# Block inverses of a recurrent scan: one product with a masked sum, ScalarE copies in place of VectorE adds, and two directions interleaved on the array

## The chip, the cores and the metric

The kernel runs on one core of a Trainium2 chip. The metric is the device time of one execution in microseconds (us). Three runs of the kernel before gave 3592.19, 3597.78 and 3598.36 us; their median, 3597.78 us, is the time before.

## The reference, cut to what matters

The program computes three transformer blocks on a sequence of 512 tokens of width 1024. The third has a recurrent mixer with 8 heads of width 64 in two directions over 528 positions (16 leading ones and 512 tokens). In each direction and head a 64x64 state S obeys, from one position to the next,

```python
def rwkv7_step(S, inp):
    r, w, k, v, kk, kka = inp
    sa = jnp.einsum('dbhij,dbhj->dbhi', S, -kk)
    S = S * w[..., None, :] + sa[..., :, None] * kka[..., None, :] + v[..., :, None] * k[..., None, :]
    y = jnp.einsum('dbhij,dbhj->dbhi', S, r)
    return S, y
```

The kernel takes 64 positions at once (a chunk). Within a chunk the values `sa` solve a triangular 64x64 system, whose matrix is I minus the strictly triangular matrix N of products of `kk` and `kka`. So each chunk needs, for 8 heads and 2 directions, the inverse P of such a matrix. It is the same for any state, and is worked out one chunk ahead of its use.

## The kernel before, in words

The program is one hand-ordered stream of instructions for each engine, tied by semaphores. Matrix products of the large projections take most of it; the change is in one stage, `RwkvScan` (lines 2345 to 2654), whose instructions lie between 2780.74 us and 3017 us of the profiled span.

The stage has one step for the 16 leading positions (called chunk -1, one direction only) and eight for the chunks 0 to 7. `steps()` gives pairs (c, n): in one step the state is carried over chunk c, while the matrices and the inverse of chunk n = c + 1 are made. The pairs are (none, -1), (-1, 0), (0, 1), ... (6, 7), (7, none).

A head is a 64x64 matrix, so a product of heads uses a quarter of the 128x128 array: which one is fixed by the half of the partitions (0 to 63 or 64 to 127) that the operands lie in and by the half that the result goes to. The trace writes such an operation as 64*64. Each float32 product shows as two matmul rows, so the 16 products of a group for both directions (4 columns of heads, 2 halves, 2 directions) are "x32", and those of one direction "x16". `quads` (line 2366) lists, for each direction and half, where the channels lie (F) and where the positions lie (t): in direction 0 both are in the same half, in direction 1 in opposite ones. A product from F to t thus uses all four quarters over the two directions, while one from t to t uses two, the two on the diagonal.

The order of TensorE in a step (line 2527 on), with the lines of the products: `grams` makes N and its transpose (2448, 2459); `right_side` (2468, 2474, 2478) and `early_sums` (2486, 2488) serve chunk c; `below` (2513) and `doubled` (2520, 2523) are a level of the inverse of chunk n, and there are five levels (block sizes 2, 4, 8, 16, 32); between the first ones stand `solution` (2493) and `late_sums` (2500, 2502) of chunk c, `pairs` with k (2459) and `fill`, which transposes three operands by products with the identity (2440).

A level before the change, per direction: `below` makes N P; VectorE multiplies it by the level's mask into `c_y` (line 2588); `doubled` makes P y (2520) and the same for the transposed inverse (2523); VectorE adds both products to `c_p` (lines 2595 and 2597). The last level makes only the first and adds it into `c_pf`. All products are from t to t.

VectorE also masks the grams (2568), adds the identity to the inverse of block size 2 and its transpose, four additions (2581), updates the state (2605, 2609), and from chunk 4 on adds the outputs (2618). ScalarE copies the right side, the solution and the transposed operands out of the accumulators (2384), the outputs of chunks 0 to 3 (2410), and after chunk -1 does two sigmoids.

Of the kernel before, what the change touches and what calls it, by code (L numbers as in the profile page):

```python
# [1305 lines left out]
class LowerBounds(Stage):  # L1306


    def dve(self, K, P):
# [4 lines left out]
        P.e.tensor_tensor(t[:, 16:24], b, m, ALU.subtract).then_inc(P.sem("lb_shifted"), P.adds("lb_shifted"))  # L1314
        P.e.wait_ge(P.sem("lb_exp"), P.due("lb_exp"))
# [7 lines left out]
    def act(self, K, P):  # L1323
        P.e.wait_ge(P.sem("lb_shifted"), P.due("lb_shifted"))
        P.e.activation(K.lbt[:, 8:24], K.lbt[:, 8:24], ACT.Exp).then_inc(P.sem("lb_exp"), P.adds("lb_exp"))
# [216 lines left out]
class BiasTable(Stage):  # L1542
# [4 lines left out]
    def dve(self, K, P):  # L1547
# [8 lines left out]
        P.e.reduce_sum(K.lamt[:, 0:2], K.lam_prod[:, :].rearrange("p (a c) -> p a c", a=2), AX.X).then_inc(P.sem("lambda_dots"), P.adds("lambda_dots"))  # L1556
        P.e.wait_ge(P.sem("lambda_exps"), P.due("lambda_exps"))
# [4 lines left out]
    def act(self, K, P):  # L1562
        P.e.wait_ge(P.sem("lambda_dots"), P.due("lambda_dots"))
        P.e.activation(K.lamt[:, 2:4], K.lamt[:, 0:2], ACT.Exp).then_inc(P.sem("lambda_exps"), P.adds("lambda_exps"))
# [780 lines left out]
class RwkvScan(Stage):  # L2345
# [35 lines left out]

    def act(self, K, P):
        def take(dst, bank, half, n):
            return P.e.activation(dst[:, 0:n, :, :], self.two(K, bank, half, n), ACT.Copy)

# [6 lines left out]
        for c, n in self.steps():  # L2392
            if c is not None:
# [6 lines left out]
                if c < 0:  # L2400
                    finish_loads(K, P, K.loads3d)
                    P.e.activation(K.z_gate[:, 0, :], K.z_gate[:, 0, :], ACT.Sigmoid)
                    P.e.activation(K.z_gate[0:32, 1, :], K.z_gate[0:32, 1, :], ACT.Sigmoid)
                    P.e.preload_act_table_set("natural_log_exp_and_others")
                if c == 7:
                    start_loads(K, P, K.loads3e)
                if 0 <= c < 4:
                    P.e.wait_ge(P.sem("state_ready"), P.due("state_ready", 0))
                    for d in range(2):
                        last = P.e.activation(K.ys[:, :, self.tokens(c, d)], self.two(K, 4, 1, 2)[:, d], ACT.Copy)  # L2410
                    last.then_inc(P.sem("y_taken"), P.adds("y_taken"))
            if n is not None:
                m = self.dirs(n)
# [6 lines left out]
    def pe(self, K, P):  # L2420
# [84 lines left out]
        def one_way(n, d):  # L2505
            return [(F, t, q, 64 * q) for q in range(4) for e, F, t in self.quads(n) if e == d]
# [1123 lines left out]
```

## Time and profile before

| | |
|---|---|
| median of three runs | 3597.78 us |
| lowest, highest run | 3592.19, 3598.36 us |
| span of the profiled execution | 3592.5 us |
| own time of the profiled execution | not recorded apart from its span |
| TensorE busy | 3438.7 us, 96% |
| VectorE busy | 1946.5 us, 54% |
| ScalarE busy | 1275.7 us, 36% |
| mean granted TensorE clock | 0.988 of full speed |

The rows of the trace have the start in us, the duration in us, the engine (PE is TensorE's matmuls, PEld its weight loads, DVE is VectorE, ACT is ScalarE), the line, the operation, what it writes and reads, the shape and the count. In brackets stands how long the engine was idle before it, and what released it.

### The profile page before, as it was taken

The page shows a single profiled execution, that of the slowest core. Times are in us where ns is not written, and L with a number is a line of the kernel's source. Part 1 is how long each engine was busy: PE and PEld are TensorE (multiplying, and loading weights), DVE is VectorE, ACT ScalarE, POOL GpSimd, SP SyncE. Part 2 cuts the span into 40 slices and gives each one's busy share as a digit, 9 for nine tenths or more (in the row PEclk, how much of TensorE's full clock was granted, in tenths as well). Part 3 has the DMA queues.
Part 4 walks back from the last instruction along what each step waited for, and adds up shares of the span by engine and source line. Part 5 has one row for each costly group of instructions (what it writes and reads, how often), then busy time and mean ns, then how long its engine had stood idle before and what let it go on. Part 6 is the DMA issues. An engine that isn't in the chain of part 4 may idle for free.

```text
span 3592.5 us, 54754 instructions
## 1 busy us (share of the span) xinstructions
PE 3438.7 (96%) x22789; PEld 2842.5 (79%) x22789; DVE 1946.5 (54%) x2646; ACT 1275.7 (36%) x1637; POOL 0.2 (0%) x4
## 2 busy tenths in 40 slices
PE   9999999999999999999999989999899888999998
PEld 7788888887788877778887768888787886888887
DVE  4566736436574654575344455344667666755434
ACT  3474424334442332453223343222532113643223
POOL 0000000000000000000000000000000000000000
PEclk9999999999999999999999999999999999999999
DMA  4102222221123222113222212222224001122221
GB/s 157 59 1 94 94 99 100 94 94 47 59 94 105 94 86 94 58 59 99 100 94 94 93 48 93 101 99 94 92 98 148 18 4 32 66 82 98 98 97 70
DMA packets 50429, 297.06 MB, mean 83 GB/s; under 512 B 6847, under 2 KB 7871, under 8 KB 17348
## 3 DMA queue, kind: packets, MB, share of 16 engines
q1 hardware_dynamic: 39376, 269.92, 22.1%
q10 hardware_dynamic: 10868, 24.41, 1.9%
q8 instruction: 148, 2.42, 0.3%
q14 instruction: 37, 0.30, 0.0%
HBM read 283.99 MB, written 10.33 MB: 82 GB/s over the span
## 4 chain that ended last, share of the span: by engine, by line
PE 87%; DVE 8%; ACT 3%; issue 1%; DMA 0%; ACTq 0%; DVEq 0%
PE PS L353 14%; PE PS L354 14%; PE PS L355 14%; PE PS L478 7%; PE PS L479 7%; PE PS L480 7%; PE PS L1995 2%; PE PS L1996 2%; PE PS L1997 2%; PE PS L2520 1%; PE PS L1300 1%; PE PS L1280 1%; PE PS L2523 1%; PE PS L2513 1%; PE PS L3012 1%
## 5 line engine op out<-in xcount | busy, mean ns | idle before, releaser
L172 DVE TENSOR_TENSOR WL<-W,WH 128x2048 fp32r<-128x2048 f32 x249 | 570.7, 2292 | 685.8 <-ACT WH L162 680.1
L162 ACT ACTIVATE WH<-W 128x2048 fp32r<-128x2048 f32 x249 | 476.3, 1913 | 1059.5 <-PE PS L480 553.3
L353 PE MATMUL PS<-XH,WH 128*128 128x512 f32 x2144 | 838.1, 391 | 4.3 <-issue 4.3
L355 PE MATMUL PS<-XH,WL 128*128 128x512 f32 x2144 | 835.2, 390 | 0.0
L354 PE MATMUL PS<-XL,WH 128*128 128x512 f32 x2144 | 835.1, 390 | 0.0
L353 PEld LDWEIGHTS PS<-XH,WH 128*128 128x128 f32 x2144 | 403.1, 188 | 94.0 <-issue 10.6
L354 PEld LDWEIGHTS PS<-XL,WH 128*128 128x128 f32 x2144 | 403.2, 188 | 84.2 <-issue 1.0
L355 PEld LDWEIGHTS PS<-XH,WL 128*128 128x128 f32 x2144 | 403.0, 188 | 84.1
L752 DVE TENSOR_TENSOR PS<-PS,R 128x512 f32<-128x512 f32 x248 | 171.0, 696 | 445.1 <-PE PS L355 440.8
L478 PE MATMUL PS<-HH,WH 128*128 128x512 f32 (+1 forms) x960 | 374.6, 390 | 1.2
L479 PE MATMUL PS<-HL,WH 128*128 128x512 f32 (+1 forms) x960 | 373.6, 389 | 0.0
L480 PE MATMUL PS<-HH,WL 128*128 128x512 f32 (+1 forms) x960 | 373.5, 389 | 0.0
L478 PEld LDWEIGHTS PS<-HH,WH 128*128 128x128 f32 x960 | 180.2, 188 | 43.0 <-issue 5.8
L480 PEld LDWEIGHTS PS<-HH,WL 128*128 128x128 f32 x960 | 180.2, 188 | 37.4
L479 PEld LDWEIGHTS PS<-HL,WH 128*128 128x128 f32 x960 | 180.2, 188 | 37.0
L1028 ACT ACTIVATE CV<-PS,params 128x512 f32<-128x512 f32 x88 | 68.0, 780 | 228.4 <-DVE PS L752 228.4
L1995 PE MATMUL PS<-XHM,WH 128*128 128x264 f32 (+1 forms) x416 | 138.4, 333 | 7.7 <-DVE slots L2199 7.7
L1996 PE MATMUL PS<-XLM,WH 128*128 128x264 f32 (+1 forms) x416 | 136.8, 329 | 0.0
L1997 PE MATMUL PS<-XHM,WL 128*128 128x264 f32 (+1 forms) x416 | 136.5, 328 | 0.0
L478 PE MATMUL PS<-XH,WH 128*128 128x512 f32 x256 | 100.2, 392 | 1.0 <-issue 1.0
L479 PE MATMUL PS<-XL,WH 128*128 128x512 f32 x256 | 99.9, 390 | 0.0
L480 PE MATMUL PS<-XH,WL 128*128 128x512 f32 x256 | 99.8, 390 | 0.0
(490 smaller groups left out, 4577.9 us busy)
## 6 DMA issues: line engine op xcount, KB each, us to landing
W<-in_weights SPq DMA_DIRECT2D x254, 1024.0 KB, 4.9
gate_spill<-slots ACTq DMA_DIRECT2D x16, 256.0 KB, 2.0
gates<-gate_spill ACTq DMA_DIRECT2D x2, 2048.0 KB
x_spill<-X ACTq DMA_DIRECT2D x1, 2048.0 KB, 8.8
X<-x_spill ACTq DMA_DIRECT2D x1, 2048.0 KB
out<-X ACTq DMA_DIRECT2D x8, 256.0 KB, 2.1
W<-in_weights SPq DMA_DIRECT2D x2, 512.0 KB, 5.2
X<-in_x ACTq DMA_DIRECT2D x4, 256.0 KB, 7.5
```

What stands on the lines that cost most here:

```text
L162: P.e.activation(K.WH[:, s, :], K.W[:, s, :], ACT.Copy).then_inc(P.sem("hi_ready"), P.adds("hi_ready"))
L172: P.e.tensor_tensor(K.WL[:, s, :], K.W[:, s, :], K.WH[:, s, :].bitcast(F32), ALU.subtract).then_inc(P.sem("weights_split"), P.adds("weight ...
L353: P.e.matmul(out, wh[:, k, c], xh[:, k, r], start=(k == 0), stop=False)
L354: P.e.matmul(out, wh[:, k, c], xl[:, k, r], start=False, stop=False)
L355: last = P.e.matmul(out, wl[:, k, c], xh[:, k, r], start=False, stop=(k == KT - 1))
L478: P.e.matmul(out, K.WH[:, s, c], h, start=(first and kk == 0), stop=False)
L479: P.e.matmul(out, K.WH[:, s, c], l, start=False, stop=False)
L480: last = P.e.matmul(out, K.WL[:, s, c], h, start=False, stop=(last_panel and kk == 1))
L752: P.e.tensor_tensor(ps, ps, K.RB[:, :], ALU.mult).then_inc(P.sem("tile_scaled"), P.adds("tile_scaled"))
L1995: P.e.matmul(out, wh[:, k, c], K.XHM[:, k, r], start=(k == 0), stop=False)
L1996: P.e.matmul(out, wh[:, k, c], K.XLM[:, k, r], start=False, stop=False)
L1997: last = P.e.matmul(out, wl[:, k, c], K.XHM[:, k, r], start=False, stop=(k == KT - 1))
```

## The change

What it does:

- `below`, `doubled` and their order: the mask of a level now includes the diagonal, and `c_n` is N + I, so that the masked product y is I plus the block, and P y is the new inverse itself. Nothing has to be added: ScalarE copies the new inverse (`grown`) and its transpose (`turned`) out of the accumulators.
- In direction 1 the intermediate product and the transposed inverse lie in the other half of the partitions (`seat`), so `below` and `grown` of direction 1 use the two quarters off the diagonal. `grown_beside_below` alternates the products of `grown` of one direction with those of `below` of the other.
- `turned` writes to the banks 2 and 3, and `grams` makes 8 further products (16 rows) that put the first transposed matrix of direction 1 into that other half.
- VectorE's order: `begin` masks `c_n` first, and adds the identity in three wide additions (in both directions at once) in place of four; the mask of the first level stands before that of `c_rb`; all additions to `c_p` and `c_pf` are gone.
- ScalarE's order: the copies of the inverse stand between those it had; the sigmoids of the step c = -1 stand at the end of the step.
- Four semaphores of short exponentials elsewhere become two by shared names. This alters no order.

The core of the diff (as it was, with parts left out):

```diff
@@ act
+        def grown(d, final=False):
+            dst = K.c_pf if final else K.c_p[:, 0]
+            P.e.wait_ge(P.sem("inverse_done"), P.due("inverse_done"))
+            P.e.activation(dst[:, d, :, :], self.two(K, 0, 0, 2)[:, d], ACT.Copy).then_inc(P.sem("inverse_ready"), P.adds("inverse_ready"))
+
+        def turned(d):
+            P.e.wait_ge(P.sem("turned_done"), P.due("turned_done"))
+            P.e.activation(K.c_p[:, 1, d, :, :], self.two(K, 2, 1, 2)[:, d], ACT.Copy).then_inc(P.sem("turned_ready"), P.adds("turned_ready"))
+
+        def level(n):
+            for d in range(n):
+                grown(d)
+                turned(d)
...
+            if n is not None:
+                level(self.dirs(n))
...
             if n is not None:
                 m = self.dirs(n)
+                level(m)
                 P.e.wait_ge(P.sem("rows_done"), P.due("rows_done"))
                 take(K.c_bT, 6, 0, m)
+                if full:
+                    level(m)
+                else:
+                    grown(0, True)
                 take(K.c_kT, 6, 1, m).then_inc(P.sem("rows_ready"), P.adds("rows_ready"))
+                if full:
+                    level(m)
+                    grown(0, True)
+                    grown(1, True)
                 P.e.wait_ge(P.sem("rows_done"), P.due("rows_done"))
                 take(K.c_v, 6, 0, m).then_inc(P.sem("rows_ready"), P.adds("rows_ready"))
@@ pe
             for d, F, t, q, cols in each(c):
                 mm(K.PS[t, d, cols], src(c, d, "a", F, q), src(c, d, "b", F, q), start=True, stop=True)
+                if d:
+                    mm(K.PS[F, 0, 256 + 64 * q:320 + 64 * q], src(c, d, "a", F, q), src(c, d, "b", F, q), start=True, stop=True)
             pairs(c, "b", "a")
...
+        def grown_beside_below(n, d, first=False):
+
+            P.e.wait_ge(P.sem("below_ready"), P.due("below_ready"))
+            if not first:
+                P.e.wait_ge(P.sem("turned_ready"), P.due("turned_ready"))
+            P.e.wait_ge(P.sem("inverse_ready"), P.due("inverse_ready"))
+            for (t, h, q, at), (t2, h2, q2, at2) in zip(heads(n, d), heads(n, 1 - d)):
+                out = mm(K.PS[t, d, at:at + 64], K.c_p[h, 1, d, q, :], K.c_y[h, d, q, :], start=True, stop=True)
+                new = mm(K.PS[h2, 1 - d, at2:at2 + 64], K.c_n[t2, 1 - d, q2, :], K.c_p[t2, 0, 1 - d, q2, :], start=True, stop=True)
+            out.then_inc(P.sem("inverse_done"), P.adds("inverse_done"))
+            new.then_inc(P.sem("below_done"), P.adds("below_done"))
+
+        def turned(n, d):
+            for t, h, q, at in heads(n, d):
+                last = mm(K.PS[h, 2 + d, 256 + at:320 + at], K.c_y[h, d, q, :], K.c_p[h, 1, d, q, :], start=True, stop=True)
+            last.then_inc(P.sem("turned_done"), P.adds("turned_done"))
...
+            right_side(c)
+            early_sums(c)
+            below(n, 0)
+            solution(c)
+            grown_beside_below(n, 0, first=True)
+            late_sums(c)
+            turned(n, 0)
+            for level in range(4):
+                grown_beside_below(n, 1, first=(level == 0))
+                if level == 0:
+                    P.e.wait_ge(P.sem("grams_masked"), P.due("grams_masked", 2))
+                    pairs(n, "k", "a")
+                turned(n, 1)
+                grown_beside_below(n, 0)
+                if level == 3:
+                    break
+                turned(n, 0)
+                if level == 0:
+                    fill(("b_rows", "k_rows"), n, ("grams_masked",))
+                elif level == 2:
+                    fill(("v_rows",), n, ("rows_ready",))
+            grown(n, 1)
+            P.e.wait_ge(P.sem("inverse_ready"), P.due("inverse_ready", 2))
@@ dve
+            masked(K.c_n, self.two(K, 0, 0, n), K.c_strict[:, 0:n, :], n)
+            masked(K.c_p[:, 0], self.two(K, 6, 0, n), K.c_first[:, 1:1 + n, :], n).then_inc(P.sem("grams_masked"), P.adds("grams_masked"))
+            masked(K.c_p[:, 1], self.one(K, 0, n), K.c_first[:, 0:n, :], n).then_inc(P.sem("dve_order"), P.adds("dve_order"))
+            eye = K.c_eye[:, :].rearrange("p (a n) -> p a n", a=1).broadcast_to([128, 4 * n, 64])
+            wide = lambda x: x[:, 0:n].rearrange("p d q n -> p (d q) n")
+            P.e.wait_ge(P.sem("dve_order"), P.due("dve_order", 0))
+            e.tensor_tensor(wide(K.c_n), wide(K.c_n), eye, ALU.add)
+            e.tensor_tensor(wide(K.c_p[:, 0]), wide(K.c_p[:, 0]), eye, ALU.add).then_inc(P.sem("inverse_ready"), P.adds("inverse_ready", n))
+            e.tensor_tensor(wide(K.c_p[:, 1]), wide(K.c_p[:, 1]), eye, ALU.add)
...
             begin(m)
+            below(m, 0)
             if full:
                 masked(K.c_rb[n % 2], self.two(K, 6, 1, m), K.c_incl[:, 0:m, :], m).then_inc(P.sem("grams_masked"), P.adds("grams_masked"))
-            below(m, 0)
-            doubled(m)
...
             below(m, 1)
             if full:
                 masked(K.c_rk, self.two(K, 6, 1, m), K.c_incl[:, 0:m, :], m).then_inc(P.sem("grams_masked"), P.adds("grams_masked"))
-            doubled(m)
             below(m, 2)
-            doubled(m, not full)
             if full:
                 below(m, 3)
-                doubled(m)
                 below(m, 4)
-                doubled(m, True)
```

## Rows read from the trace of the kernel before

**Rows 1.** The page: its head.

```profile
span 3592.5 us, 54754 instructions
```

**Rows 2.** The page: chain of work that ended last, by engine.

```profile
PE 87%; DVE 8%; ACT 3%; issue 1%; DMA 0%; ACTq 0%; DVEq 0%
```

**Rows 3.** Timeline: first product of steps n = -1, 0, 1, and of the last.

```profile
2780.74 0.54 PEld L2448 LDWEIGHTS PS<-c_meta 64*64 64x64 f32 x16 [1.77 <-ACTq L101]
...
2797.92 0.69 PE L2448 MATMUL PS<-ar 64*64 64x64 f32 x32 [0.58 <-ACT c_v L2384]
...
2821.84 0.69 PE L2448 MATMUL PS<-ar 64*64 64x64 f32 x32 [0.52 <-DVE c_pf L2597]
...
3010.76 1.15 PE L2468 MATMUL PS<-c_v,c_ak 64*64 64x64 f32 x32 [0.52 <-DVE c_pf L2597]
```

**Rows 4.** Timeline of one step (c = 2, n = 3) from its start, products and masks.

```profile
2876.05 0.56 PEld L2448 LDWEIGHTS PS<-ar 64*64 64x64 f32 x32 [0.66 <-DVE c_pf L2597]
...
2876.51 0.87 PEld L2459 LDWEIGHTS PS<-ar 64*64 64x64 f32 x32
...
2877.34 1.06 PEld L2468 LDWEIGHTS PS<-c_v,c_ak 64*64 64x64 f32 x32
...
2877.69 1.29 DVE L2568 TENSOR_TENSOR c_p<-PS,masks 128x512 f32<-128x512 f32 x2 [1.69 <-PE PS L2459]
...
2879.20 0.60 PEld L2478 LDWEIGHTS PS<-c_s,ar 64*64 64x64 f32 x32
...
2879.61 1.43 DVE L2581 TENSOR_TENSOR c_p<-c_p,wide_consts 128x256 f32<-128x256 f32 x4
...
2880.65 1.02 PEld L2513 LDWEIGHTS PS<-c_p,c_n 64*64 64x64 f32 x32
```

**Rows 5.** The same step: the state's update and the wait behind it.

```profile
2886.71 0.69 DVE L2605 TENSOR_TENSOR c_s<-c_s,PS 128x512 f32<-128x512 f32 x1 [0.75 <-PE PS L2502]
...
2889.30 0.55 PEld L2520 LDWEIGHTS PS<-c_y,c_p 64*64 64x64 f32 x16 [1.06 <-DVE c_y L2588]
```

**Rows 6.** The same step: the operands' transposes and one level.

```profile
2891.11 1.07 PEld L2440 LDWEIGHTS PS<-square_consts,ar 64*64 64x64 f32 x64
...
2892.09 1.02 PEld L2513 LDWEIGHTS PS<-c_p,c_n 64*64 64x64 f32 x32
...
2893.38 0.54 PEld L2520 LDWEIGHTS PS<-c_y,c_p 64*64 64x64 f32 x16 [0.27 <-DVE c_y L2588]
...
2895.71 1.16 PEld L2513 LDWEIGHTS PS<-c_p,c_n 64*64 64x64 f32 x32
```

**Rows 7.** Timeline: from a product through VectorE's mask to the next product.

```profile
2873.64 0.54 PEld L2513 LDWEIGHTS PS<-c_p,c_n 64*64 64x64 f32 x16 [0.40 <-DVE c_p L2597]
...
2874.37 0.42 DVE L2588 TENSOR_TENSOR c_y<-PS,masks 128x256 f32<-128x256 f32 x1 [0.45 <-PE PS L2513]
...
2874.84 0.55 PEld L2520 LDWEIGHTS PS<-c_y,c_p 64*64 64x64 f32 x16 [0.20 <-DVE c_y L2588]
```

**Rows 8.** ScalarE's copies: the 128x256 one by groups, a wide one and its reader.

```profile
L2410 ACT ACTIVATE ys<-PS 128x256 f32<-128x256 f32 x8 | 2.6, 381 | 16.7 <-DVE c_s L2609 16.7
...
3015.54 0.60 ACT L2384 ACTIVATE c_u<-PS 128x512 f32<-128x512 f32 x1 [1.55 <-PE PS L2493]
...
3016.19 0.56 PEld L2500 LDWEIGHTS PS<-c_rb,c_u 64*64 64x64 f32 x32 [0.84 <-ACT c_u L2384]
```

**Rows 9.** Waits of TensorE from 2780 to 3020 us: one cause.

```profile
PE PS L2493 <- issue: 2.4, 4, 0.8
```

**Rows 10.** Step n = -1: the product behind VectorE's longest queue.

```profile
2791.50 0.67 PEld L2520 LDWEIGHTS PS<-c_y,c_p 64*64 64x64 f32 x16 [2.79 <-DVE c_y L2588]
```

**Rows 11.** Stretches: from:to, length, PE, PEld, DVE, ACT, POOL busy, clock, DMA.

```profile
2790.00:2792.00 2.00, 0.49 (x14) 0.50 (x16) 1.45 (x3) 0.00 (x0) 0.00 (x0) 0.97 0.13 16
2792.00:2794.00 2.00, 2.00 (x44) 2.00 (x42) 0.75 (x2) 0.00 (x0) 0.00 (x0) 0.50 0.86 287
...
2877.00:2904.00 27.00, 24.55 (x930) 23.44 (x924) 17.29 (x42) 3.54 (x7) 0.00 (x0) 1.00 0.02 4
```

More of the change, by code:

```diff
@@ L2392, in act @@
         for c, n in self.steps():
+            full = n is not None and n >= 0
             if c is not None:
@@ L2503, in late_sums @@
             last.then_inc(P.sem("state_done"), P.adds("state_done"))
-        def one_way(n, d):
-            return [(F, t, q, 64 * q) for q in range(4) for e, F, t in self.quads(n) if e == d]
-        def below(n):
-            for d in range(self.dirs(n)):
-                P.e.wait_ge(P.sem("inverse_ready"), P.due("inverse_ready"))
-                for F, t, q, at in one_way(n, d):
-                    last = mm(K.PS[t, d, at:at + 64], K.c_n[t, d, q, :], K.c_p[t, 0, d, q, :], start=True, stop=True)
-                last.then_inc(P.sem("below_done"), P.adds("below_done"))
@@ new lines, in below, with grown @@
+        def below(n, d):
+            P.e.wait_ge(P.sem("inverse_ready"), P.due("inverse_ready"))
+            for t, h, q, at in heads(n, d):
+                last = mm(K.PS[h, d, at:at + 64], K.c_n[t, d, q, :], K.c_p[t, 0, d, q, :], start=True, stop=True)
+            last.then_inc(P.sem("below_done"), P.adds("below_done"))
+        def grown(n, d, first=False):
+            P.e.wait_ge(P.sem("below_ready"), P.due("below_ready"))
+            if not first:
+                P.e.wait_ge(P.sem("turned_ready"), P.due("turned_ready"))
+            for t, h, q, at in heads(n, d):
+                last = mm(K.PS[t, d, at:at + 64], K.c_p[h, 1, d, q, :], K.c_y[h, d, q, :], start=True, stop=True)
+            last.then_inc(P.sem("inverse_done"), P.adds("inverse_done"))
@@ L2539, in pe @@
                 continue
-            below(n)
-            if c is not None:
-                solution(c)
-            doubled(n)
-            if c is not None:
-                late_sums(c)
-            P.e.wait_ge(P.sem("grams_masked"), P.due("grams_masked", 2 if full else 1))
-            pairs(n, "k", "a")
-            below(n)
-            doubled(n)
-            fill(("b_rows", "k_rows"), n, ("grams_masked",))
-            below(n)
-            doubled(n, not full)
-            fill(("v_rows",), n, ("rows_ready",))
@@ L3160, in level @@
         return (row // (2 * b) == col // (2 * b)) & (lo // b % 2 == 0) & (hi // b % 2 == 1)
-    masks = [strict[d] for d in (1, 0, 1)] + [level(d, 1) for d in (1, 0, 1)] + [level(d, b) for b in (2, 4, 8, 16, 32) for d in range(2)]
+    masks = [strict[d] for d in (1, 0, 1)] + [level(d, 1) for d in (1, 0, 1)] + [level(d, b) | (row == col) for b in (2, 4, 8, 16, 32) for d in range(2)]
     more = [strict[d] | (row == col) for d in range(2)] + [row == col]
```

102 lines of the change are left out of this document (43 added, 59 removed).

## The prediction

> **What bounds the kernel now.** The head of the page gives the span, 3592.5 us [rows 1]. It is 0.15% below the median of the runs, 3597.78 us, so a difference worked out in the profile is subtracted from the median as it stands. The chain of work that ended last is 87% TensorE, 8% VectorE, 3% ScalarE [rows 2]; nearly all of TensorE's part lies in projections that the change doesn't touch. The timeline then finds the stage: its first product starts at 2780.74, the first of step n = 0 at 2797.92, of n = 1 at 2821.84, of the last step at 3010.76 [rows 3]. So step n = -1 takes 17.18 us, n = 0 23.92, and the seven steps n = 1 to 7 188.92, 26.99 each. The last step has no inverse and is unchanged.
>
> Inside a step TensorE is the bound by instructions rather than by waits: 24.55 us busy of 27, at the full clock (1.00, the 2.4 GHz level) [rows 11]. What a group costs depends on its quarters. Between 2879.20 and 2880.65 stand three groups of 32 rows between channels and positions (four quarters): 0.48 us each, and `grams` takes 0.46 for 32. Two groups of 32 from t to t (two quarters) take 1.86 us from 2877.34 to 2879.20, 0.93 each [rows 4]; 16 such rows hence take 0.46. The inverse is of that kind: a level in steady state lasts 2895.71 - 2892.09 = 3.62 us [rows 6] with 96 such rows, 2.8 us, besides 0.47 of a transposing group and waits. VectorE sets the end only in the opening (masks, additions) and behind the state's update, where TensorE waits 1.06 us [rows 5].
>
> **The change, walked through one step** (c = 2, n = 3; times from its start).
>
> *Opening.* `grams` gets 16 more rows, on the diagonal, which direction 0 uses too: 32 rows for two quarters, 0.93 instead of 0.46. With the 0.83 of line 2459 [rows 4] it ends at 1.76. VectorE started 1.64 after the step's start [rows 4], now 2.1. Three masks take 2877.69 to 2879.61, 1.92 us [rows 4], as before: 4.0. Then the wide additions replace four of 128x256, which took 1.43. No row has a 128x512 addition out of SBUF; it lies between one narrow one, 0.42, and two, 0.84 [rows 7], and I take the 0.69 of line 2605, same size [rows 5]. The first two are needed: 1.3, inverse ready at 5.35 (4.9 to 5.7). TensorE arrives at 1.76 + 3.31 = 5.07, so it waits 0.3.
> `below` for one direction 0.46, `solution` 0.93: 6.75. The alternating group has 32 rows on all four quarters, the pattern and banks of the `grams` group: 0.46, 7.2. `late_sums` needs ScalarE's copy of the solution. Before, 64 rows of `doubled` (1.86 us) covered it. A product group's start to the reader's start is about 0.73 for 16 rows in two quarters [rows 7], ScalarE's wide copy 0.60 and 0.05 to the reader [rows 8]: 7.6, so 0.4 of wait is uncovered. Late sums 0.95, `turned` 0.46: 9.0. Alternating group 0.46, `pairs` 0.83: 10.3.
>
> *Middle.* Before, VectorE's update of the state began at 2886.71, 10.66 after the start. Now it can begin at 8.8. From there to the product that it held up were 2.59 us [rows 5], of which a wide mask takes 0.64, a level's mask and its reader 0.47 [rows 7], leaving 1.5: ready at 10.3. So the wide mask of the second grams waits for `pairs` (10.3 + 0.35 = 10.65), and the next alternating group starts at 10.65 + 0.64 + 0.47, about 11.7. TensorE idles 1.0 there. VectorE then has this direction's mask, the other's at 11.7 + 0.73 (to 12.9) and the mask of `c_rk` (to 13.5), which frees the bank for `fill`: a new wait of 0.9, since `turned` ended at 12.65. Fill takes 0.98 [rows 6]: 14.5.
>
> *Levels.* From here each half level is latency: group start to mask 0.73, mask and reader 0.47, together 1.20 (2873.64 to 2874.84) [rows 7]. ScalarE's copy beside it is no later: 0.73 + 0.38 [rows 8] + 0.05 to 0.12. `turned` (0.46) and its copy fit in the next half. Three halves: 18.15; then `turned`, fill of v and start of the next, 1.45; two more halves: 22.0 for the last `grown`. It ends the step with 0.73, then ScalarE: the last inverse and behind it the copy of v, which `grams` waits for, 0.3 + 0.60 + 0.05. Step: 23.7. To this come pauses without a releaser ("issue"), 2.4 us over the stage at `solution` alone [rows 9], 0.3 a step; both ends for a step are 0 and 0.8, I take 0.6: 24.3. From c = 4, VectorE adds outputs before the wide mask, two of 128x256 at 0.34 and 0.42 by the four of 1.43 [rows 4]: 0.76, of which 0.35 is slack in the wait for `pairs`: 0.4 for three steps.
>
> *Sum.* Seven steps: 188.9 - 7 x 24.3 - 1.2 = -17.6 us. Step n = 0 has a shorter opening (one direction of c): by the same walk 23.0, -0.9. Its two sigmoids move behind its copies, under the next opening, where ScalarE has nothing to do until the right side is ready at 4.4: they cost nothing, and about 1 us once if that cover fails. Step n = -1: VectorE's long split of a weight panel stood behind `doubled` and held TensorE 2.79 us [rows 10]; now it runs beside `doubled`. -2.4, bounds 0 and -4. The added ScalarE work, 18 copies of 0.38 in a step, is on an engine that was busy 3.54 of 27 us [rows 11]. The two renamed semaphores cost nothing: same order. Total -20.9 us: 3577 us.
>
> **One rule against it.** In the `grams` group, two quarters of different row halves write the same bank, and four run together at 0.46 us for 32 rows [rows 4]. The Trainium skill ("TensorEngine Tiling (Array Packing)", section "Gotcha 1: PSUM Pressure") says that different row tiles cannot access the same bank at once. By that rule the alternating group, which has both halves in each of two banks, would gain nothing over two quarters; the trace disagrees, and so it is a rival with a small chance.
>
> **Rivals.**
> *The alternating groups don't overlap (slower).* Place: nine groups a step. Price: 0.93 in place of 0.46; eight are on the path, 3.7 us a step, 30 us: 3607 us. From 5.6 slow groups of the nine no gain is left, and from 7.5 it is slower by over 0.2%. For it: the mixed order (two products of different kinds) is in no row. Against it: the `grams` rows. Chance 0.04.
> *The clock falls in the new gaps.* The longest wait of the steady steps in the rows is 1.06 us [rows 5]. Now it works 0.9 us in the last 2.9 of a step, and idles twice in the middle. In step n = -1 the clock was 0.97 while TensorE was busy 0.49 of 2 us, and then 0.50 (the 1.2 GHz level) over the next 2 us, in which it was busy throughout [rows 11]. The row bounds the length of such a fall by 2 us from below; taken as 3, an estimate, half is lost, 1.5. At the end of seven steps that is 10.5: 3588 us, still faster. Chance 0.20. In two places of each step it would be 21, no change, 3598: 0.05.
> *ScalarE becomes the releaser.* If its copy comes 0.2 late in each half level, 9 x 0.2 x 8 = 14: 3591, within the bound of no change by a hair. Chance 0.05.
> *More comes.* If pauses vanish in the new waits and fill isn't held: 0.6 + 0.9 in seven steps, 10 more: 3566. Chance 0.10.
> That the change doesn't do what it says: the counts in the diff match (10 groups of `below`, 10 of `grown`, 8 of `turned` in a step, as before), so no chance of its own.
>
> **Numbers.** Forecast 0.56, the rivals 0.44. About 0.2% (7.2 us) is what a measurement of this kernel can tell from no change. Faster: 0.56 + 0.20 + 0.10, 0.86; same 0.09; slower 0.05. The range reaches from 3566 to the clock's case, 3589.
>
> **What would show it.** Steps of about 24.3 us instead of 27.0; the alternating lines 0.46 us from group to group's end; half levels 1.2 us apart, released by `c_y` of VectorE; a wait of `late_sums` for ScalarE near 0.4; one of `fill` near 0.9; the first `below` waiting 0.3 for the addition; TensorE's busy time in a step near 19 us. A clock under 1.00 in stretches at the start of steps would show the clock's case; alternating groups of 0.93 the rule; a longest wait on a copy, ScalarE's. Anything outside the stage that moved would make the prediction wrong in kind.

## The result, and the profile after

Nine executions of each kernel, alternating on one chip: 3606.17 us median after the change (3599.68 to 3614.0), 3595.45 before (3591.19 to 3598.36). The ratio is 1.0033 [1.0024, 1.0042]: the change makes the kernel slower by 10.7 us. 3577 us were forecast.

The page of the kernel after: its head, busy time by engine, and the chain by engine.

```profile
span 3604.0 us, 55035 instructions
...
PE 3425.8 (95%) x22917; PEld 2825.3 (78%) x22917; DVE 1897.2 (53%) x2490; ACT 1329.1 (37%) x1786; POOL 0.2 (0%) x4
...
PE 87%; DVE 8%; ACT 3%; issue 1%; DMA 0%; ACTq 0%; DVEq 0%
```

TensorE is busy 13 us less than before, although it has 128 product rows more, and the span is 11.5 us longer: what was saved in busy time came back as idle time, and more. The timeline of the kernel after says where. These rows correspond to [rows 3]: the first product of step n = -1, of n = 0, of n = 1, and of the last step.

```profile
2782.23 0.56 PE L2478 MATMUL PS<-c_meta 64*64 64x64 f32 x12 [1.34 <-ACTq L101]
...
2796.51 0.35 PE L2478 MATMUL PS<-ar 64*64 64x64 f32 x8 [0.57 <-ACT c_v L2388]
...
2824.29 0.50 PE L2478 MATMUL PS<-ar 64*64 64x64 f32 x8 [1.06 <-ACT c_v L2388]
...
3023.40 1.15 PE L2500 MATMUL PS<-c_v,c_ak 64*64 64x64 f32 x32 [1.02 <-ACT c_pf L2393]
```

Step n = -1 takes 14.3 us (17.18 before), n = 0 27.8 (23.92), the seven steps n = 1 to 7 199.1 (188.92). That is -2.9, +3.9 and +10.2, together +11.2 of the 11.5 us between the two spans: the difference lies in the stage, and nearly all of it in the steady steps.

For these I compare stretches of six steps in the view by stretches. Each runs from ScalarE's copy of `c_v` in step n = 0 to the same copy six steps later; that copy lies some 6 us ahead of a step's end before the change and at its end after it, which leaves the mean step as it is. The columns are those of [rows 11]. First the kernel before, then the one after.

```profile
2815.50:2977.55 162.05, 143.71 (x5384) 136.25 (x5382) 105.15 (x251) 19.90 (x39) 0.00 (x0) 1.00 0.02 4
```

```profile
2823.56:2993.86 170.30, 131.82 (x5472) 121.20 (x5472) 68.88 (x136) 61.81 (x151) 0.00 (x0) 0.97 0.02 4
```

The mean step is 27.0 us before and 28.4 after. TensorE's busy time fell by 2.0 us a step and VectorE's from 17.5 to 11.5, much as the change means it to. A step has 897 product rows before and 912 after (5384 and 5472 by six). Now the waits in these two stretches, first before, then after (us in total, times, longest).

```profile
PE PS L2520 <- DVE c_y L2588: 7.4, 7, 1.6
PE PS L2448 <- DVE c_pf L2597: 3.1, 6, 0.5
PE PS L2493 <- issue: 2.4, 4, 0.8
...
PE PS L2513 <- issue: 1.1, 2, 0.7
```

```profile
PE PS L2478 <- ACT c_v L2388: 6.6, 6, 1.3
PE PS L2562 <- issue: 4.5, 7, 1.0
PE PS L2470 <- DVE c_rk L2626: 4.2, 6, 0.7
PE PS L2561 <- issue: 4.2, 5, 1.4
PE PS L2561 <- DVE c_y L2645: 4.0, 5, 1.1
PE PS L2551 <- DVE c_y L2645: 3.4, 6, 0.6
PE PS L2568 <- issue: 2.9, 4, 1.1
PE PS L2470 <- issue: 1.7, 2, 0.9
...
```

Waits for an engine grew from 12.1 us to 19.4 over six steps, foreseen in kind. The rows "issue", in which TensorE waits for nothing that the profile shows, grew from 5.1 to 16.6 (all rows summed), which wasn't foreseen. I call these rows pauses. One step of the kernel after (c = 1, n = 2, from 2852.63 to 2879.83) shows where they stand.

```profile
2852.63 0.35 PE L2478 MATMUL PS<-ar 64*64 64x64 f32 x8 [1.06 <-ACT c_v L2388]
...
2860.31 0.57 PE L2532 MATMUL PS<-c_rb,c_u 64*64 64x64 f32 x23 [0.24 <-ACT c_u L2388]
...
2861.32 0.38 PE L2532 MATMUL PS<-c_rb,c_u 64*64 64x64 f32 x9 [0.44 <-issue]
...
2865.23 0.39 PE L2568 MATMUL PS<-c_p,c_y 64*64 64x64 f32 x7 [1.08 <-issue]
...
2867.36 1.16 PE L2470 MATMUL PS<-square_consts,ar 64*64 64x64 f32 x64 [0.69 <-DVE c_rk L2626]
...
2868.96 0.21 PE L2561 MATMUL PS<-c_y,c_p 64*64 64x64 f32 x1 [0.33 <-issue]
```

Two more, of 0.42 and 1.01 us, follow at 2872.67 and 2876.47. The five pauses make 3.3 us of this step of 27.20 us. They come every 3.8 us, in the middle of groups (after 23 of the 32 rows of line 2532), whatever the line. That spacing has one counterpart in the profile: the queue of instruction packets. Its row for the stretch 2823.56 to 2993.86 of the kernel after (packets, MB, share):

```profile
q8 instruction: 43, 0.70, 1.7%
```

43 packets of 16 KB in 170.3 us: one per 3.96 us. 5472 product rows and 5472 weight loads in 43 packets are 254.5 instructions in each, so I take 256 to a packet, 64 bytes each: 128 product rows with their weight loads. The kernel before has 42 in 162.05 us, one per 3.86 us:

```profile
q8 instruction: 42, 0.69, 1.8%
```

Hence the theory that I put to the test, called FEED in the expectations: TensorE's instructions arrive at a rate of about one packet per 3.4 to 4 us, 27 to 31 ns a product row. In two quarters a row takes 29 ns [rows 4], so by this theory the kernel before ran at the rate of arrival and showed hardly a pause; in four quarters it takes 14.4 ns, and then TensorE outruns its instructions. Its rivals: WAITS, the longer chain of copies and masks sets the step and the pauses are incidental; and the clock, which was at its lower level at some step starts (below).

### The profile page after: what moved, and what is told of

Read it like the earlier page. It is cut to its first block, busy times and chain, and to the rows that moved or that the text cites. A ratio compares the mean times of both kernels' runs of the same rounds, so it can differ in the third digit from the quotient of the medians.

```text
span 3604.0 us, 55035 instructions
## 1 busy us (share of the span) xinstructions
PE 3425.8 (95%) x22917; PEld 2825.3 (78%) x22917; DVE 1897.2 (53%) x2490; ACT 1329.1 (37%) x1786; POOL 0.2 (0%) x4
## 4 chain that ended last, share of the span: by engine, by line
PE 87%; DVE 8%; ACT 3%; issue 1%; DMA 0%; ACTq 0%; DVEq 0%
PE PS L353 14%; PE PS L355 14%; PE PS L354 14%; PE PS L478 7%; PE PS L480 7%; PE PS L479 7%; PE PS L1995 2%; PE PS L1996 2%; PE PS L1997 2%; PE PS L1300 1%; PE PS L1280 1%; PE PS L2561 1%; PE PS L3053 1%; PE PS L3055 1%; PE PS L3054 1%
```

## The experiments

Each difference is to the kernel before on the same chip; the kernel after stands at +10.7 us. The last five columns are of a six-step stretch, cut in the same way; pauses, waits and the time at half clock are us over the six steps. The stretch is of one execution, which for `in_turn` lay 4.2 us and for `tuned` 4.5 us below the median of its kernel, so their mean steps may be on the low side. The run `feed` has no row: it was executed once, at 3695.74 us, and only its trace is read.

| kernel | median us | ratio to before | difference | mean step | product rows a step | pauses | other waits | time at half clock |
|---|---|---|---|---|---|---|---|---|
| before | 3595.45 | | | 27.0 | 897 | 5.1 | 12.1 | 0 |
| after | 3606.17 | 1.0033 [1.0024, 1.0042] | +10.7 | 28.4 | 912 | 16.6 | 19.4 | 10.2 |
| wide_turned | 3596.14 | 0.9999 [0.9990, 1.0008] | +0.5 | 27.1 | 816 | 9.4 | 21.7 | 13.7 |
| in_turn | 3604.96 | 1.0025 [1.0016, 1.0035] | +9.4 | 28.3 | 912 | 8.2 | 19.7 | 10.2 |
| warm_ends | 3605.63 | 1.0027 [1.0018, 1.0036] | +10.0 | 28.1 | 918 | 18.7 | 10.0 | 0 |
| before_more | 3621.16 | 1.0074 [1.0058, 1.0089] | +26.2 | 29.8 | 1025 | 17.2 | 12.6 | 0 |
| wide_before | 3587.58 | 0.9977 [0.9967, 0.9986] | -7.4 | 25.7 | 801 | 2.0 | 10.3 | 0 |
| wide_all | 3578.55 | 0.9946 [0.9930, 0.9961] | -16.4 | 24.7 | 600 | 2.6 | 22.3 | 3.4 |
| tuned | 3596.14 | 0.9999 [0.9990, 1.0008] | +1.2 | 27.1 | 914 | 24.5 | 8.4 | 3.4 |
| in_place | 3589.70 | 0.9992 [0.9983, 1.0001] | -2.3 | 26.2 | 897 | 4.2 | 8.3 | 0 |
| before_tuned | 3584.60 | 0.9981 [0.9972, 0.9990] | -7.4 | 26.0 | 897 | 1.9 | 8.2 | 0 |
| wide_in_turn | 3577.13 | 0.9957 [0.9942, 0.9973] | -14.8 | 24.2 | 600 | 0.8 | 23.2 | 0 |

### feed: the rate by itself

Four blocks of 384 products each, with nothing to wait for, stand ahead of the stage's first step; their results are not used.

```diff
         P.e.wait_ge(P.sem("meta_staged"), P.due("meta_staged"))
+        H = self.HALVES
+        for i in range(384):
+            mm(K.PS[H[(i // 2) % 2], 6 + (i % 2 != (i // 2) % 2), 0:64], K.c_meta[H[i % 2], 0, 0, :], K.c_meta[H[i % 2], 1, 0, :], start=True, stop=True)
+        for i in range(384):
+            mm(K.PS[H[i % 2], 6, 0:64], K.c_meta[H[i % 2], 0, 0, :], K.c_meta[H[i % 2], 1, 0, :], start=True, stop=True)
...
```

The third block has 8 columns on four quarters, the fourth 128.

> The kernel after with four blocks of 384 extra 64x64 products ahead of the scan (1536 TensorE rows each, a weight load and a matmul counted as one row each; results unused): (1) four quarters, 64 columns; (2) two quarters, 64 columns; (3) four quarters, 8 columns; (4) four quarters, 128 columns. Theory FEED (TensorE's instructions arrive at no more than 256 rows, one 16 KB instruction packet, in about 3.4 us, 13.3 ns a row): block 1 about 20 us, block 2 about 22 us, block 3 about 20 us, block 4 about 20 us, and packets 3.4 us apart in all four. Theory ARRAY (the rate of short bursts, 0.46 us for 32 matmul rows in four quarters, holds): block 1 about 11 us, block 2 about 22 us, block 3 below 11 us, block 4 about 20 us; packets 1.9 us apart in block 1.

The timeline of the first block (four quarters, 64 columns, 768 product rows):

```profile
2781.70 2.66 PE L2574 MATMUL PS<-c_meta 64*64 64x64 f32 x164 [1.34 <-ACTq L101]
2785.73 2.09 PE L2574 MATMUL PS<-c_meta 64*64 64x64 f32 x128 [1.36 <-issue]
2789.20 2.09 PE L2574 MATMUL PS<-c_meta 64*64 64x64 f32 x128 [1.38 <-issue]
2793.22 2.09 PE L2574 MATMUL PS<-c_meta 64*64 64x64 f32 x128 [1.93 <-issue]
2796.96 2.09 PE L2574 MATMUL PS<-c_meta 64*64 64x64 f32 x128 [1.65 <-issue]
2800.98 1.56 PE L2574 MATMUL PS<-c_meta 64*64 64x64 f32 x91 [1.93 <-issue]
```

The four blocks by stretches (the clock is the third column from the end):

```profile
2781.70:2802.30 20.60, 12.36 (x765) 11.66 (x768) 0.00 (x0) 1.91 (x1) 0.00 (x0) 1.00 0.18 56
2802.30:2826.90 24.60, 23.31 (x788) 22.74 (x780) 0.00 (x0) 0.00 (x0) 0.00 (x0) 1.00 0.02 5
2826.90:2848.10 21.20, 19.34 (x778) 18.95 (x778) 0.00 (x0) 0.00 (x0) 0.00 (x0) 0.58 0.02 5
2848.10:2870.60 22.50, 22.50 (x772) 22.27 (x771) 0.00 (x0) 0.00 (x0) 0.00 (x0) 0.94 0.02 4
```

This shows what FEED says, if not at the 3.4 us that it named: bursts of exactly 128 rows, 2.09 us each, then a pause, 3.81 us from burst to burst on average ((2800.98 - 2785.73) / 4), with no semaphore in sight. The block takes 20.6 us, 27 ns a row, where 768 rows at 14.4 ns would be 11. The second block (two quarters) took 24.6 us, the third, of 8 columns and at a mean clock of 0.58, 21.2, the fourth, of 128, 22.5. The second and the fourth had been expected at 22 and 20 by both theories and don't tell them apart; the first and the third do. An eighth of the columns isn't done sooner, and a clock near the lower level doesn't make it later: it is the number of instructions that counts. Two quarters lose only 4 us to four.

The trace also holds the start and the end of each packet's transfer, and they tie the pauses to the packets. In the first block the transfers end at 2784.17, 2787.86, 2791.81, 2795.64 and 2799.62, and the five bursts start 1.56, 1.34, 1.41, 1.32 and 1.36 us later. In the stretch of the kernel after, each of the 24 pauses ends 1.27 to 1.59 us after the end of a transfer. Over the stretches of all twelve kernels of the table and this block there are 174 pauses, and all end 1.18 to 1.60 us after one, while waits for an engine end at any distance from it. So what TensorE waits for in a pause is its packet. In the kernel after, the next transfer starts 1.04 to 2.03 us after the row that ends a pause, never sooner, and takes 0.88 to 1.50 us. Transfer, arrival and the first rows thus stand one behind the other, and no two packets of the kernel after start less than 3.34 us apart.

### wide_turned, wide_all and wide_in_turn: fewer instructions, same chain

The products of `turned` for four heads become one of 256 columns with the weights of the first head, so the transposed inverse isn't what is to be computed; groups, semaphores, copies and masks stay. `wide_all` does the same to the alternating groups as well, so the inverse isn't either. `wide_in_turn` is `wide_all` with the alternating groups issued one kind after the other.

```diff
         def turned(n, d):
-            for t, h, q, at in heads(n, d):
-                last = mm(K.PS[h, 2 + d, 256 + at:320 + at], K.c_y[h, d, q, :], K.c_p[h, 1, d, q, :], start=True, stop=True)
+            for t, h, q, at in heads(n, d)[0:2]:
+                last = mm(K.PS[h, 2 + d, 256:512], K.c_y[h, d, q, :], K.c_p[h, 1, d, :, :], start=True, stop=True)
```

> The kernel after, in which the 8 products of a turned group are 2 products of 256 columns each: the same columns, banks and quarters, 24 TensorE rows fewer in each of 8 groups of a step (192 rows a step of some 1850). The transposed inverse is not computed by this. Theory FEED: 192 x 13.3 ns = 2.6 us less in each of 8 steps, 20 us in all, a ratio to before near 0.9975. Theory WAITS (the steps are long by the chain of TensorE, VectorE and ScalarE and by the clock alone): the group was hidden, nothing changes, ratio 1.003.

> The kernel after, in which turned groups and the alternating groups are products of 256 columns (2 in place of 8, 4 in place of 16): the same columns, quarters and banks, 192 + 432 TensorE rows a step fewer, some 1200 in place of 1824. The inverse isn't computed by this. Theory FEED: the rows no longer bind, and a step falls to what the walk through its waits gave, 23.7 to 24.5 us in place of 28.4: 30 us faster than the kernel after, ratio near 0.995. Theory WAITS: the walk itself is wrong (ScalarE's or VectorE's latencies are longer than rows say), and the step stays above 27 us.

`wide_turned` is 10.2 us faster than the kernel after, by 96 product rows a step that carried the same columns. WAITS foretold no gain, since the chain of copies and masks is left alone; FEED alone foretold 20. Half of it came. `wide_all`, with 312 rows fewer, is 27.1 us faster than after. Its stretch:

```profile
2822.62:2970.76 148.14, 120.56 (x3600) 90.16 (x3600) 68.97 (x136) 62.32 (x152) 0.00 (x0) 0.99 0.01 3
```

Pauses are down to 2.6 us over six steps, and the step is 24.7 us; the predicted walk gave 23.7 without pauses and 24.3 with them. With instructions out of the way, the walk of the prediction holds to 0.6 us or better.

### in_turn: without the alternation

The order of the 32 rows alone is changed.

```diff
-            for (t, h, q, at), (t2, h2, q2, at2) in zip(heads(n, d), heads(n, 1 - d)):
+            for t, h, q, at in heads(n, d):
                 out = mm(K.PS[t, d, at:at + 64], K.c_p[h, 1, d, q, :], K.c_y[h, d, q, :], start=True, stop=True)
+            for t2, h2, q2, at2 in heads(n, 1 - d):
                 new = mm(K.PS[h2, 1 - d, at2:at2 + 64], K.c_n[t2, 1 - d, q2, :], K.c_p[t2, 0, 1 - d, q2, :], start=True, stop=True)
```

> The kernel after, with the two products of each alternating group issued one direction after the other (16 rows on two quarters, then 16 on the other two) instead of alternating; the same instructions and waits. Theory FEED: the burst is slower by 0.46 us but the instructions that follow are then there in time, so part of it comes back: 5 to 20 us slower than the kernel after. Theory WAITS: nine groups x 0.46 us x 8 steps, 30 us slower, ratio 1.011. If the next half's products overlap with the first's because the quarters differ: below 5 us.

It costs nothing that can be measured: +9.4 against +10.7 us. In the trace the 32 rows of a group start within 0.71 to 0.76 us in nearly all groups, where the alternating ones do within 0.43 to 0.64, so the burst is some 0.2 us longer and not the 0.46 expected. Its stretch:

```profile
2820.17:2989.78 169.61, 140.40 (x5472) 131.42 (x5472) 68.99 (x136) 61.07 (x151) 0.00 (x0) 0.97 0.02 4
```

TensorE is busy 8.6 us longer than after over six steps, and the pauses are 8.4 us shorter: one for the other, since the next packet comes when it comes. The part of the change that its name speaks of, the alternation, is worth nothing here.

> The kernel wide_all (1200 TensorE rows a step, the inverse not computed), with the products of each alternating group issued one direction after the other. Both theories of the rows agree that here they don't bind. Theory OVERLAP LOST: nine groups are 0.46 us longer, eight of them on the path, 3.7 us a step, 25 to 30 us slower than wide_all, ratio near 1.003; then what the alternation is worth was hidden in the real kernel by the arrival of the rows. Theory QUARTERS OVERLAP BY THEMSELVES (TensorE starts the second direction's products, on free quarters, while the first's run): under 5 us slower than wide_all, and the alternation is worth nothing in any kernel.

`wide_in_turn` asks it again where instructions don't bind. It isn't slower than `wide_all` either (-14.8 against -16.4 us, intervals that overlap). In the trace of `in_turn` rows of line 2563 begin from 2868.26 on among those of 2561 (2867.96 to 2868.43), which were issued before them: products on free quarters overlap to a part by themselves.

### warm_ends: the clock

In the kernel after the granted clock falls at some step starts (from:to, length, then PE, PEld, DVE, ACT and POOL busy, then the clock).

```profile
2824.00:2828.00 4.00, 3.71 (x94) 3.74 (x96) 0.12 (x1) 3.89 (x5) 0.00 (x0) 0.57 0.00 0
...
2876.00:2880.00 4.00, 1.88 (x67) 1.64 (x69) 0.42 (x1) 1.64 (x4) 0.00 (x0) 0.84 0.02 4
2880.00:2884.00 4.00, 4.00 (x94) 4.00 (x95) 0.42 (x1) 0.00 (x0) 0.00 (x0) 0.50 0.02 4
```

In a stretch in which TensorE was busy 1.88 of 4 us the clock falls, at 2878.7, and it is at its 1.2 GHz level (0.50) for all of the next 4 us, in which only 94 rows run. By the clock's own records in the trace the six-step stretch of the kernel after has two falls, one of 3.4 and this one of 6.8 us, of which 5.7 lie in the step n = 3, the longest of the seven (30.25 us). The 17 us of the expectation don't hold for these steps. Three products on the whole array around the last `grown` fill that end:

```diff
+            mm(K.PS[:, 4, 0:256], K.ident, K.reset[:, 0:256], start=True, stop=True)
             grown(n, 1)
+            for _ in range(2):
+                mm(K.PS[:, 4, 0:256], K.ident, K.reset[:, 0:256], start=True, stop=True)
```

> The kernel after, with three unused products of 128x128 by 256 columns in the waits at the end of each of the eight steps (one before the last grown, two behind it; 6 rows of matmul and 6 of weights a step more), so that TensorE is busy there. Theory CLOCK (falls of the granted clock in the openings cost about half their length, some 17 us of half clock more than before): no falls within the steps, 8 us faster than the kernel after, ratio near 1.001. Theory FEED alone: no gain, slightly slower by 12 rows a step and by what delays the last grown.

The same stretch of a step's start, in `warm_ends`:

```profile
2824.00:2828.00 4.00, 4.00 (x123) 3.50 (x121) 0.67 (x2) 3.75 (x6) 0.00 (x0) 1.00 0.01 4
```

The falls are gone from the steady steps, and the time isn't (+10.0 us). The clock's case did happen, and its 10.2 us at half speed are at most 5.1 us of work. Removed, they brought 0.5 us, while the pauses rose from 16.6 to 18.7 us: a faster TensorE waits longer for its packet. The 6 rows a step that the fillers add cost by FEED 1.3 us. Each interval is some 3 us wide to either side, so a gain of a few us can't be excluded; that the clock makes the 10.7 us can.

### before_more and wide_before: is the kernel before bound by arrival?

`before_more` adds to the old kernel 64 products of 8 columns a step, on quarters that are free, in the groups of `doubled`; nothing waits for them. `wide_before` has the old kernel's second product of `doubled` as one of 256 columns, so that the transposed inverse isn't what is to be computed.

```diff
                 for F, t, q, at in one_way(n, d):
+                    if more:
+                        o = slice(64 - t.start, 128 - t.start)
+                        mm(K.PS[t, 2 + d, 256:264], K.c_y[o, d, q, :], K.c_y[o, d, q, 0:8], start=True, stop=True)
                     last = mm(K.PS[t, d, at:at + 64], K.c_p[t, 1, d, q, :], K.c_y[t, d, q, :], start=True, stop=True)
```

> The kernel before, with 64 extra products a step of 8 columns each (results unused), one ahead of each product of line 2520 from the second level on, on the two quarters that this group leaves idle: 256 TensorE rows a step more and next to no array time. Theory FEED (256 rows need 3.4 to 3.9 us wherever they run): 8 steps x 3.4 us, some 20 to 27 us slower, ratio 1.006 to 1.0075, and the pauses without a releaser grow by that. Theory ARRAY (the kernel before is bound by its two quarters and its waits, and the pauses are incidental): under 5 us slower.

> The kernel before, in which the 8 products of line 2523 of a direction are 2 products of 256 columns: same columns, quarters and banks, 192 TensorE rows a step fewer. The transposed inverse isn't computed by this. Theory FEED alone: 192 x 13.4 ns = 2.6 us a step, 20 us faster, ratio 0.9943. Theory BALANCE (two quarters at 14.4 ns a row pass no faster than the rows arrive at 13.4 to 14.5, so before is bound by both at once): only the pauses go, 0.85 us a step, 5 to 8 us faster, ratio 0.998.

The stretch of `before_more`, its largest pauses, and its packets there:

```profile
2818.01:2996.70 178.69, 146.80 (x6151) 137.63 (x6147) 105.33 (x250) 19.94 (x38) 0.00 (x0) 1.00 0.02 4
```

```profile
PE PS L2513 <- issue: 5.6, 6, 1.5
PE PS L2493 <- issue: 4.3, 4, 1.5
```

```profile
q8 instruction: 48, 0.79, 1.9%
```

+26.2 us for 8 x 128 product rows is 25.6 ns a row, for products that TensorE can do beside others: its busy time grew by 3.1 us over six steps, the step by 2.8 us each. The pauses of the kernel after appear in the old one as soon as it has more instructions. The other way, 96 rows fewer a step give 7.4 us, where 27 ns a row would be 20.7. So the kernel before stands at the point of balance: more instructions cost in full, and fewer bring a third. The reason that I give for the third, execution on two quarters as the next bound, is argued from its busy time (140.58 of 154.31 us) and not tested.

### tuned, in_place and before_tuned: what can be had

`tuned` is the change with its waits taken out: VectorE masks direction 0 of the second level ahead of the mask of `c_ak`, and direction 1 behind that of `c_rk`; ScalarE copies v before the last two levels end; and 32 rows that need only the state (line 2474, now `from_state`) move from the opening to the end of the step before, where TensorE waited for `c_v`. The products of `c_v` with `c_rk` take their place in the opening.

```diff
+            from_state(n)
             grown(n, 1)
...
+            if full:
+                below(m, 1, (0,))
             P.e.wait_ge(P.sem("grams_done"), P.due("grams_done"))
...
-            below(m, 1)
+                below(m, 1)
             if full:
                 masked(K.c_rk, self.two(K, 6, 1, m), K.c_incl[:, 0:m, :], m).then_inc(P.sem("grams_masked"), P.adds("grams_masked"))
+                below(m, 1, (1,))
```

> The kernel after with three reorderings and no work left out: ScalarE copies v before the last two levels' copies; VectorE masks the first direction of the second level ahead of c_ak, and c_rk ahead of the second direction; the products of the state with r of the next chunk stand ahead of the last grown of the step. Waits of TensorE for others are 3.2 us a step in the kernel after. Theory FEED with a shallow buffer (while TensorE waits, at most about one packet is fetched ahead, so waits and rows add up): each microsecond of wait removed is a microsecond less, 2 us a step, 14 to 18 us faster than the kernel after, ratio 0.998. Theory FEED with a deep buffer (only the rows count): the time doesn't change.

```profile
2815.48:2978.03 162.55, 127.83 (x5486) 117.37 (x5482) 68.96 (x136) 61.44 (x150) 0.00 (x0) 0.99 0.02 4
```

```profile
PE PS L2569 <- issue: 5.6, 7, 1.5
PE PS L2568 <- issue: 5.3, 5, 1.9
PE PS L2575 <- issue: 4.9, 5, 1.2
```

```profile
q8 instruction: 43, 0.70, 1.9%
```

The waits fell by 11 us over six steps, the pauses rose by 8, and 9.5 us were gained over the whole kernel by the medians instead of the 14 or more expected (14.6 by the spans of the two profiled executions; the eleven runs of `tuned` lie between 3588.79 and 3599.43 us). TensorE now stands 4.1 us of each step for its packets, 3.78 us apart, as in `feed` (3.81): 914 rows are 7.14 packets, and 7.14 x 3.78 = 27.0 us is the step, by the way the distance was counted. As long as the packets come 3.8 us apart, 912 rows need as long as the old kernel's step, in whatever order.

`in_place` is `tuned` with one edit more: all products stay from t to t, so on two quarters, without the 16 added rows, and `below` is issued ahead of `grown`.

```diff
-        return t if d == 0 else slice(64 - t.start, 128 - t.start)
+        return t
...
-                if d:
-                    mm(K.PS[F, 0, 256 + 64 * q:320 + 64 * q], src(c, d, "a", F, q), src(c, d, "b", F, q), start=True, stop=True)
```

> The kernel tuned without the other seat of direction 1: all products of the inverse from t to t on two quarters, the two of a group one after the other (below first), and without the 8 extra gram products: 32 TensorE rows a step fewer, 1795 as in the kernel before, no alternation. All of the result is computed. Theory FEED (rows at 3.4 to 3.9 us for 256 set the step, quarters don't): 32 x 14.8 ns = 0.5 us a step less than tuned, 4 us, ratio 0.9987. Theory QUARTERS (alternation over four quarters is worth 0.46 us nine times a step): 15 to 30 us slower than tuned, ratio above 1.004.

```profile
2819.34:2976.31 156.97, 141.85 (x5383) 135.81 (x5381) 68.78 (x136) 63.99 (x151) 0.00 (x0) 1.00 0.02 4
```

It gives the quarters back and is no slower for it, by the medians 3.4 us faster than `tuned` (the intervals of the ratios overlap). Busy time is up by 14 us over six steps, pauses are down from 24.5 to 4.2.

`before_tuned` leaves the inverse of the old kernel as it was and takes only the moves: `from_state`, the split masks, and in step n = -1 `doubled` ahead of the split of the weight panel.

```diff
             below(m, 0)
-            doubled(m)
-            if c is None:
+            if c is not None:
+                doubled(m)
+            else:
...
                 split_dve(K, P)
                 P.split_left -= 1
+                doubled(m)
...
+                from_state(n)
                 P.e.wait_ge(P.sem("inverse_ready"), P.due("inverse_ready", 2))
```

> The kernel before with its additions, and three reorderings alone: VectorE's split of the weight panel in step n = -1 ahead of its additions; the first mask of the second level ahead of c_ak, behind the state's update; the products of the state with r at the end of the step before. Theory FEED: the steps are within 0.5 us of the time of their rows (1795 rows at 14.8 ns, 26.5 us, against 27.0), so 0 to 4 us come from the steps and 3 us from step n = -1: 3 to 7 us faster than before, ratio 0.9985. Theory WAITS (2.0 us of wait a step, no other bound): 10 us and more from the steps, ratio below 0.997.

```profile
2812.86:2969.15 156.29, 145.05 (x5384) 137.42 (x5382) 104.70 (x251) 19.90 (x39) 0.00 (x0) 1.00 0.02 5
```

3584.6 us, ratio 0.9981 [0.9972, 0.9990]: faster than both kernels, and of those that compute all of the reference the fastest. With -7.4 us it came out just beyond the 3 to 7 us that FEED gave. 3 us of it are step n = -1, 14.2 us instead of 17.2. The rest, 4.4 us by the medians and 6.8 by the spans, is more than the 0 to 4 that FEED allowed the steps: its packets come 3.72 us apart, those of the kernel before 3.86, so removed waits do shorten a step that has hardly a pause.

## Why the prediction was wrong, by its own steps

**The step that failed** is the term of the pauses, "To this come pauses without a releaser ("issue"), ... 0.3 a step; both ends for a step are 0 and 0.8, I take 0.6". They measured 2.8 us a step (16.6 / 6). The term was read as a constant of the old kernel [rows 9], when it was the first sign of a second bound that the same trace could have shown: seven packets a step, one per 3.86 us, in a step of 27. In the step n = 2 of the kernel after, the walk without pauses, 23.7, and the five pauses, 3.3, make 27.0 of its 27.20 us. Shortening what TensorE does with an instruction doesn't shorten its arrival. The predicted step of 24.3 us with 912 rows would have needed a packet per 3.4 us; `feed` has 3.8.

**Where the other part lies.** In the steady step, 27.0 to 28.4: execution (the time that is neither pause nor wait) went from 24.1 to 22.4 us, pauses from 0.85 to 2.8, waits from 2.0 to 3.2. Pauses and waits grew by 3.1 us together, execution shrank by 1.7. Arrival by itself accounts for a step as long as before plus 0.5 us (the 15 added rows); that the step is longer by 1.4 I put down to the waits, which aren't fully hidden by the arrival going on beside them. `tuned` bears this out: without 1.8 us of the waits a step, 1.3 of it came back. Against the 24.3 us predicted, the mean step is 4.1 us too long: 2.2 are pauses beyond the 0.6, the slow clock is at most 0.9, and about 1 us a step is assigned to nothing.

**What was right.** Step n = -1: -2.9 for -2.4 predicted. The alternating groups: 32 rows start within 0.43 to 0.64 us (0.46 predicted, 0.93 by the rival), so the rival of groups that don't overlap fell. By the rule of the Trainium skill ("TensorEngine Tiling (Array Packing)", "Gotcha 1: PSUM Pressure") they would have taken 0.93; the trace disagrees. VectorE began 2.1 us after the step's start as walked, and the first `below` 5.36 us (the inverse ready at 5.35); no row shows the wait of 0.3 before it. The wait for the mask of `c_rk` was 0.69 (0.9), for `c_u` 0.24 (0.4). A half level as latency, 1.20, is 1.27 in VectorE's masks of the kernel after, where no pause falls between them:

```profile
2869.68 0.42 DVE L2645 TENSOR_TENSOR c_y<-PS,masks 128x256 f32<-128x256 f32 x1 [2.37 <-PE PS L2562]
2870.95 0.42 DVE L2645 TENSOR_TENSOR c_y<-PS,masks 128x256 f32<-128x256 f32 x1 [0.84 <-PE PS L2562]
2872.22 0.42 DVE L2645 TENSOR_TENSOR c_y<-PS,masks 128x256 f32<-128x256 f32 x1 [0.84 <-PE PS L2562]
```

The end of the step waits 1.06 for ScalarE's `c_v`; 0.3 + 0.60 + 0.05 were walked. TensorE's busy time near 19 us a step was not met: 22.0. I put this down to the slower clock and to modelled ends of rows that reach into pauses; nothing tests it.

**What was half right.** The clock's case had a chance of 0.25 in its two forms and came true as a fact of the trace: two falls in the six steps, of 3.4 and 6.8 us where 3 had been taken, at a price of at most 5.1 us together. It isn't the cause: `warm_ends` removes it and gains 0.5 us. ScalarE as a releaser of half levels wasn't seen; its copies follow in time.

**Slips that changed nothing.** The saving of the seven steps is written as a difference with a minus sign, 188.9 - 170.1 - 1.2 = 17.6. Of the two groups "from t to t" in [rows 4] the second, line 2474, goes from channels to channels; it also uses two quarters. The longest wait of the steady steps before was 1.6 us (line 2520), not 1.06.

**Step n = 0** took 27.8 us instead of 23.0 predicted. In its first 3.5 us the clock is near the lower level:

```profile
2796.50:2800.00 3.50, 3.49 (x86) 3.50 (x88) 0.00 (x0) 0.00 (x0) 0.00 (x0) 0.54 0.02 5
```

A second fall follows at 2803.6; together 6.8 us of the step are at half clock. Its first `below` waits 2.3 us for VectorE's addition (1.9 in the kernel before), and 1.3 us are pauses. This is read from the trace; no run tests this step by itself.

**Left open.** What makes the next transfer start 1.04 us after a pause in one case and 2.03 in another, and so what sets the spacing of the packets between 3.4 and 4.0 us in `feed`. A way to fewer instructions that still computes the reference (operands laid so that several products share their weights) wasn't tried; `wide_all`, which computes something else, came to 16 us below the kernel before.

## What to carry to other kernels

Before making small products run side by side, count TensorE's instructions: packets of the instruction queue in the stretch, times their spacing, is a floor that no overlap lowers. Here the spacing was 3.81 us in a row of pure products, and 3.72 in the best whole stretches (`before_tuned`, `before_more`). Where pauses without a releaser come at equal distances in the middle of groups, that floor is near; here only fewer instructions (wider products) and moved waits helped. A steady step that shows few such pauses can still stand right at it, so test by adding free instructions before shortening their execution.

## What the runs showed of the hardware that was not expected

- TensorE's instructions of small products arrive at 256 (128 weight loads, 128 product rows) per 3.4 to 4.0 us, 3.81 on average in the first block of `feed`, 27 to 30 ns a product row, whether the product has 8 or 64 columns (21.2 and 20.6 us for 768 rows).
- A pause without a releaser ends 1.18 to 1.60 us after the transfer of a packet of q8 ends (174 of 174), and in the kernel after the next transfer starts no sooner than 1.04 us after it.
- Four quarters sustain 14.4 ns a row only within a packet (2.09 us for 128 rows, their tail included). The Trainium skill ("TensorEngine Tiling (Array Packing)", its opening paragraph) says that several smaller tiles in place of the one array give smaller matrices a higher throughput. Over 128 rows the trace agrees (2.09 us, where two quarters at 29 ns a row would take 3.7); over 768 rows little of it is left (20.6 against 24.6 us).
- Products issued one kind after the other on different quarters overlap to a part without alternating: `wide_in_turn` is no slower than `wide_all`.
- A granted clock of 0.50 to 0.57 over 4 us at some step starts cost nothing that could be measured in steps that wait for their instructions (`warm_ends`, 0.5 us, intervals of some 3 us to either side).
